# Two plain gate tiles instead of four ahead of a layer's pairs, and one more gate pair, in a two-layer conv and retention trunk

## What is computed

```python
h = rmsnorm(x, g);  p = h @ w_in                 # 1024 x 9216
hc, b, c, z_a, q, k, v, z_r, g_a, g_r = split(p)
u = c * hc;  conv = causal 3-tap convolution of u
a = ((b * conv) * silu(z_a)) @ w_a
o = chunked retention of rotary(q), rotary(k), v, normalised per head
r = (o * silu(z_r)) @ w_r
x = x + (sigmoid(g_a) * a + sigmoid(g_r) * r) @ w_o
# after both layers: rmsnorm with final_g
```

## Time and profile before

| | before |
|---|---|
| median of 3 runs | 2304.2 us (2302.47 to 2304.54) |
| span of the profiled execution | 2304.0 us |
| PE busy | 2281.5 us, 99%, 17005 matmuls |
| DVE busy | 1377.8 us, 60% |
| POOL busy | 903.7 us, 39% |
| ACT busy | 870.1 us, 38% |
| matmuls of the pairs (L1608) in the chain that ended last | 61% of the span |
| plain tiles (L1597) in that chain | 2% |
| mean granted TensorE clock | 0.996 |

### The profile page before, as it was taken

How to read it: one execution, slowest core, us unless ns; L and a number is a source line. 1 busy time by engine, 2 the same in 40 slices (tenths; PEclk the granted TensorE clock), 3 DMA queues, 4 the chain that set the end, 5 groups by cost and what they waited for, 6 DMA issues and landing times.

```text
span 2304.0 us, 40644 instructions
## 1 busy us (share of the span) xinstructions
PE 2281.5 (99%) x17005; PEld 2260.4 (98%) x17005; DVE 1377.8 (60%) x1486; ACT 870.1 (38%) x1366; POOL 903.7 (39%) x603
## 2 busy tenths in 40 slices
PE   7999999999999999999999999999999999999998
PEld 7999999999999999999999999999999999999998
DVE  6776777556663565743476776774566526556334
ACT  6433333344444444322233333334334444333133
POOL 3555665565555300000047556554665551000000
PEclk9999999999999999999999999999999999999999
DMA  9322122233333565554452222223343326656444
GB/s 298 86 66 67 55 75 65 71 129 133 124 105 114 200 211 194 182 170 124 133 172 75 66 61 61 66 65 114 125 133 112 99 94 237 219 195 200 124 151 133
DMA packets 260519, 294.06 MB, mean 128 GB/s; under 512 B 9032, under 2 KB 218224, under 8 KB 260336
## 3 DMA queue, kind: packets, MB, share of 16 engines
q1 hardware_dynamic: 260176, 291.40, 39.0%
q10 hardware_dynamic: 160, 0.05, 0.0%
HBM read 206.84 MB, written 84.57 MB: 126 GB/s over the span
## 4 chain that ended last, share of the span: by engine, by line
PE 94%; issue 2%; POOL 1%; DVE 1%; DMA 1%; ACT 0%; SPq 0%; DVEq 0%; POOLq 0%; ACTq 0%
PE ps L1608 61%; PE ps L1650 21%; PE ps L1869 3%; PE ps L1597 2%; PE ps L1659 1%; PE ps L1657 1%; PE ps L1658 1%; PE ps L1754 1%; PE ps L1699 1%; PE ps L1688 1%; DMA w_raw<-in_w_in_dram 1%; POOL s_lo L691 0%; DVE t_lo L1145 0%; PE ps L1670 0%; PE ps L1738 0%
## 5 line engine op out<-in xcount | busy, mean ns | idle before, releaser
L1608 PE MATMUL ps<-t_hi,s_lo 128*128 128x272 f32 x3808 | 788.2, 288 | 0.0
L1608 PE MATMUL ps<-t_hi,s_hi 128*128 128x272 f32 x3808 | 787.4, 288 | 0.5 <-ACT snap L838 0.5
L1608 PE MATMUL ps<-t_lo,s_hi 128*128 128x272 f32 x3808 | 785.1, 288 | 0.0
L1608 PEld LDWEIGHTS ps<-t_hi,s_hi 128*128 128x128 f32 x3808 | 598.8, 188 | 0.9 <-issue 0.9
L1608 PEld LDWEIGHTS ps<-t_lo,s_hi 128*128 128x128 f32 x3808 | 598.4, 189 | 0.0
L1608 PEld LDWEIGHTS ps<-t_hi,s_lo 128*128 128x128 f32 x3808 | 594.4, 189 | 0.0
L1178 DVE TENSOR_TENSOR e<-ps,snap 128x544 f32<-128x544 f32 x272 | 195.9, 723 | 518.7 <-PE ps L1608 390.1
L691 POOL TENSOR_TENSOR s_lo<-w_pair,s_hi 128x512 fp32r<-128x512 f32 x136 | 229.8, 1690 | 321.5 <-ACT s_hi L828 321.5
L838 ACT ACTIVATE snap<-ps 128x544 f32<-128x544 f32 x272 | 169.2, 622 | 433.1 <-PE ps L1608 432.7
L828 ACT ACTIVATE s_hi<-w_pair 128x512 fp32r<-128x512 f32 x204 | 127.7, 629 | 169.3 <-PE ps L1608 167.2
L702 POOL TENSOR_TENSOR sA<-w_pair 128x512 f32<-128x512 f32 x68 | 89.4, 1314 | 220.3 <-DVE s_lo L1166 220.3
(11 more groups left out here) (242 smaller groups left out, 3724.4 us busy)
## 6 DMA issues: line engine op xcount, KB each, us to landing
w_pair<-in_w_in_dram SPq DMA_DIRECT2D x136, 512.0 KB, 5.0
w_raw<-in_w_o_dram SPq DMA_DIRECT2D x24, 512.0 KB, 5.2
xs<-x_keep SPq DMA_DIRECT2D x16, 544.0 KB, 5.4
prod_keep<-e SPq DMA_DIRECT2D x16, 544.0 KB, 2.7
v_keep<-e SPq DMA_DIRECT2D x16, 544.0 KB, 6.7
z_keep<-e SPq DMA_DIRECT2D x16, 544.0 KB, 3.8
prod_raw<-prod_keep SPq DMA_DIRECT2D x16, 544.0 KB, 6.4
vT<-v_keep SPq DMA_DIRECT2D x16, 544.0 KB, 7.4
```

What stands on the lines that cost most here:

```text
L1608: i = mm(ps[:, r + p, 0:PART], s[j][:, k, :], b[operand][:, k, p * PART:(p + 1) * PART], start=(FRESH[j] and k == 0 and t == 0), stop=(k = ...
```

## The change

`NG` goes from 4 to 2. Only g_a and g_r of m = 0 remain plain tiles, and ("G", 1) becomes a pair, between the last K pair and ("G", 2): a layer has 2 plain tiles and 35 pairs. All counts and waits that are written with `NG` or `NP` follow. DVE's loop over k still makes all four k of T, so its call of `gate_first` gets a condition. ACT's loops over tiles 2 and 3 become empty by their bounds, as do those of POOL and SP.

```diff
-NG = 4
+NG = 2
 PAIRS = [(kind, m) for m in range(KT) for kind in "AB"] + [(kind, h) for h in range(HEADS) for kind in "VZK"] \
     + [("G", m) for m in range(NG // 2, KT)]
 NP = len(PAIRS)
@@
                     if k:
                         combine_t(l, k)
                     low_t(l, k)
-                    gate_first(l, k)
+                    if k < NG:
+                        gate_first(l, k)
                 for j in (M3, M7, M4):
                     low_w(l, 0, j)
```

## The result

The changed kernel takes 2326.5 us in the median of 4 runs (2325.6 to 2328.3), against 2304.4 us for the kernel before in the same comparison (2302.5 to 2305.3): 1.0099 times as long, 95% interval 1.0087 to 1.0111, so 22 us slower. The forecast was 2325.8 us, between 2319.5 and 2332.

What follows compares the result with a forecast made beforehand. PE's matmuls were taken as the bound, with other engines' preparation deciding at each layer's front. A pair of 21.05 us less a front 10.3 us shorter, in two layers: 2304.2 + 21.5 + 0.1 = 2325.8 us, range 2319.5 to 2332.

Steps and rivals of the forecast that it cites:

- 6 and 7: high part for M5 to M6: Layer front, ACT and POOL alternating up to M6: 8.2 us without gate tile 3's sigmoid, plus 1.3 us of turns with low_t(3).
- end of tile 1 to M6: Sum of the front's chain after the change: 22.9 us against 33.2 before, leaving PE idle 13.8 us per layer.
- What bounds the front: After the change, preparation on DVE, ACT and POOL sets M6; removing two tiles takes their cover, but the covered work stays.
- Step 4: DVE's combine_t(3) in the front, fully overlapped by POOL's three operations: 6.0 us, bounds 2.96 and 6.2.
- Step 7: POOL in the front taking turns with DVE's low_t(3): 1.3 us, bounds 0 and 2.6.
- The wait before M5: PE in layer 0's front: M2 ends at 70.3, but M5 must wait for low_t(3), done about 71.9.
- Smaller parts: Effects around plain tile 1, including POOL's sA delaying DVE, up to 0.65 us past its end: 0.1 us in layer 0.
- Clock: PE's 8 us idle before M1 lowers the clock to about 0.5; M1's slowness lies inside the wait and costs nothing.
- The likeliest case: Both layers' fronts lose cover as summed, slow matmuls hidden in the wait: 2325.8 us, chance 0.74.
- the rival: Clock still or again down at M6, so M6 and M3 run slow: 5.6 us per layer, 2337 us, chance 0.12.
- Removed and added PE work: Four gate tiles removed, 48.1 us; two pairs added, 42.1 us: 6.0 us less if nothing waited.
- the faster one: Rival: the cover wasn't needed, T's preparation keeps up with PE, only the matmul saving shows: 2298 us, chance 0.02.
- That with little effect of POOL: Rival: front's chain nearly free of POOL, M6 4.3 us sooner per layer: 2317 us, chance 0.10.

## Why the prediction was right

The steps of the chain, in layer 1, where the trace has each as a distance between starts:

| step | predicted | measured |
|---|---|---|
| 1: DVE takes plain tile 1 | 1.26 | 1.27 (1195.86 to 1197.13) |
| 2: combine_t(2), low_t(2) | 5.51 | 5.51 (to 1202.64) |
| 4: combine_t(3) beside POOL | 6.0 | 6.08 (to 1208.72) |
| 5: ACT's next operation | 0.6 | 0.57 (to 1209.29) |
| 6 and 7: high part for M5 to M6 | 8.2 + 1.3 | 9.13 (to 1218.42) |
| end of tile 1 to M6 | 22.9 | 22.6; layer 0 23.5 |

- **What bounds the front** was right, and shown, not only argued: the matmuls put into PE's idle time cost nothing, and leaving T work out or moving ACT's order moved M6.
- **Step 4** held because a row of layer 1 had the same overlap.
- **Step 7** was the middle between bounds and came out at 0.93 instead of 1.3. Its mechanism is that of step 4: low_t(3) took 3.73 us where alone it takes 2.63.
- **The wait before M5** was expected at 1.6 us (M2 done at 70.3, low_t(3) at 71.9) and was 0.34 us in layer 0 and none in layer 1, since low_t(3) beside POOL took 3.73 us and not 5.3. This cost nothing, as M6 waited for ACT.
- **Smaller parts.** POOL's sA did collide with low_t(0) in layer 0 (3.73 us again), DVE took plain tile 1 at 53.71, 0.9 us after its end. I had put 0.1 us for this; 0.9 is more than the bound of 0.65, as plain tile 1 itself ended a microsecond earlier than in the trace of before. This is most of the 0.9 us between layer 0 and layer 1.
- **Clock.** It fell in the wait before M1 and was back in time for M5 in both layers, as predicted, and that cost nothing: with the clock up until the wait before M6 the time was the same, 2325.9. The likeliest case left out a second fall at M6, which the rival had. It came in layer 0, for 3.4 us behind M6's start, at 1.5 us, about a quarter of the rival's 5.6 us, since the clock was back before M3; in layer 1 it didn't come.
- **Removed and added PE work.** 21.04 us for a pair in layer 1; of the 24 us of the removed tiles each layer got back about 10, and the rest became idle time or slow matmuls. Nothing stalled behind the K pair.
- The **rivals**: the faster one needed M6 within 12.4 us of the plain tile and was off by 10. That with little effect of POOL fell with the 1.8 us rows.
- **Luck.** That the total came within 1 us is partly chance: the 1.5 us of clock at M6 were not in the sum, and layer 0's plain tile 1 ended 1.1 us earlier than in the trace of before, which has nothing to do with the change.

What the prediction did not see is in the kernel before. It named the 0.4 us wait before M6 as something the kernel already does, and priced it at its length. By the slower pace behind it, it costs 2.0 us per layer, five times that. The changed kernel has that pace too, so the forecast was not touched by it.

## What to carry to other kernels

Work that looks replaceable because something cheaper computes the same may be the cover of a preparation on other engines. Before shrinking it, write the chain of those engines from the point where they are released, in the order in which each one's queue is written, and compare its length with what PE has left; here 23 us against 9. Where DVE and POOL operations that each read two operands from SBUF can overlap, as here, count them as one queue, and try the cheapest experiment first: idle matmuls in the gap tell whether PE is waiting for somebody or somebody for PE.

When such a chain is nearly covered, it is worth taking the last fraction of a microsecond off it by the order in one engine's queue, as in the kernel with M1 evacuated first, the fastest of this study.

## What the runs showed of the hardware that I had not expected

- **A wait changes the pace of what follows.** Products of 24 matmuls (272 columns, each with its weight load) took 3.000 us as long as PE had gone from the plain tiles into the pairs without a wait, and 3.0067 us behind any wait (0.25 us before M6, 0.71 us put in), for 174 to 235 products, up to the end of the layer's pairs. In the next layer, after other matmuls, 3.000 came back. The pace is not a matter of the clock, which was 1.00 in both. With the 192 idle matmuls ahead of the pairs PE didn't wait either, and the pace was 3.0067 from the second product on (3.004 in the first), so a wait isn't the only way into it. In the same trace the idle matmuls, all with the same weights, ran at 3.000 per 24, and the plain tiles before them at 3.013. What holds the pace, and what in PE's queue differs between the two, stays open.
- **The same wait, two clocks.** Before M6 PE waited 2.58 us in layer 0 and 2.56 us in layer 1, and the clock fell in the first case alone; in the run with 12 us of added matmuls it fell behind 2.37 us in layer 0 and not behind 1.70 us in layer 1. Where it fell, one product took 4.6 us instead of 3.1.
